# A two-block transformer layer on one core: three opening blocks made one, tiled load of x, gate product turned round, one modulation row moved

## The reference, cut to what matters

```python
xn = rmsnorm(x, norm1_g)                       # 256 x 2048
z = xn @ w_in                                  # columns: q, k, v, o (1024 each), 8 gates, u (1024)
q, k, v, o, gates, u = split(z)
gates = gates + b_gates                        # 256 x 8
...
dt = exp(log_dt); mag = exp(lam_re * dt)       # 64 groups x 64 states
ar, ai = mag * cos(lam_im * dt), mag * sin(lam_im * dt)
# x = u * B per group; a complex recurrence over the 256 tokens; y = Re(C * state) + d * u
ys = s5_groups(u, ...)                         # then a small gated product per group
mix = concat([mlstm(q, k, v, gates, o), ys]) @ w_out
...
# second block
mod = silu(c) @ w_ada + b_ada                  # one row of 6 * 2048, from a vector of 2048
```

## Time and profile before

| | |
|---|---|
| median of 3 runs | 3634.81 us (3632.55 to 3634.88) |
| the profiled execution, its own time | 3632.39 us |
| its span | 3630.5 us |
| busy share of the span: PE, DVE, POOL, ACT | 71%, 70%, 29%, 23% |
| mean HBM traffic | 283 GB/s |

### The profile page before, as it was taken

One profiled execution on the slowest core, in us unless ns is written; L12 is line 12 of the kernel. 1 busy time (PEld: TensorE's weight loads), 2 busy tenths in 40 slices (PEclk: granted clock), 3 DMA queues, 4 the chain that ended last, 5 costly groups with the idle time before them and its releaser, 6 DMA issues. The chain is left out here.

```text
span 3630.5 us, 27099 instructions
## 1 busy us (share of the span) xinstructions
PE 2592.8 (71%) x10406; PEld 1825.1 (50%) x10406; DVE 2542.4 (70%) x2541; ACT 835.7 (23%) x763; POOL 1060.7 (29%) x642
## 2 busy tenths in 40 slices
PE   7999899200165520006557999988899999999999
PEld 4444578100022200002224888767678788888887
DVE  3665647999899789987776787666746644444565
ACT  1001244000000000000002333344433433334333
POOL 1641000668867667885661000000000000000000
PEclk9999999655577665557777999989999999999999
DMA  6787355999999999999996898334466455555775
GB/s 200 254 304 278 128 194 203 372 372 417 418 422 422 411 406 422 422 422 422 421 421 257 314 321 290 134 122 142 139 223 244 162 188 194 186 185 192 259 260 191
DMA packets 332954, 1028.57 MB, mean 283 GB/s; under 512 B 36060, under 2 KB 36572, under 8 KB 265524
## 3 DMA queue, kind: packets, MB, share of 16 engines
q1 hardware_dynamic: 259124, 490.31, 39.0%
q0 software_dynamic: 73728, 536.90, 35.8%
HBM read 1020.29 MB, written 6.86 MB: 283 GB/s over the span
## 5 line engine op out<-in xcount | busy, mean ns | idle before, releaser
L387 DVE TENSOR_TENSOR slab_low<-ring,slab_high 128x2048 fp32r<-128x2048 f32 x240 | 550.0, 2292 | 522.5 <-ACT slab_high L380 522.3
L380 ACT CAST slab_high<-ring 128x2048 fp32r<-128x2048 f32 x304 | 580.1, 1910 | 1015.8 <-PE bank L366 800.5
L2238 PE MATMUL bank<-pool,upto 128*128 128x512 f32 x256 | 187.4, 901 | 658.9 <-ACT upto L2019 522.9
L1828 POOL DMA_INDIRECT pool<-in_peer_u,pool x256 | 509.9, 1992 | 413.3 <-DVE pool L1592 248.5
L364 PE MATMUL bank<-slab_high,left_high 128*128 128x512 f32 x1568 | 617.3, 394 | 11.4 <-DVE slab_low L387 7.6
L365 PE MATMUL bank<-slab_low,left_high 128*128 128x512 f32 x1568 | 613.4, 391 | 0.0
L366 PE MATMUL bank<-slab_high,left_low 128*128 128x512 f32 x1568 | 613.1, 391 | 0.0
L1638 DVE CUSTOM_DVE_ANT_0 pool<-pool,nat 128x2048 f32<-128x2048 f32 x248 | 558.6, 2289 | 30.1 <-DMA pool<-in_peer_u,pool 29.4
L1649 DVE SCALAR_TENSOR_TENSOR res<-pool,res 128x2048 f32<-128x2048 f32 x192 | 451.5, 2351 | 131.2 <-DMA pool<-in_peer_v,pool 115.7
L1828 POOL DMA_INDIRECT pool<-in_peer_v,pool x256 | 420.7, 1644 | 227.4 <-PE bank L2238 161.8
L2238 PEld LDWEIGHTS bank<-pool,upto 128*128 128x128 f32 x256 | 72.6, 298 | 774.3 <-issue 774.3
(11 more groups left out here) (577 smaller groups left out, 2923.1 us busy)
## 6 DMA issues: line engine op xcount, KB each, us to landing
ring<-in_w_in SPq DMA_DIRECT2D x140, 1024.0 KB, 5.0
ring<-in_w_ffn_in SPq DMA_DIRECT2D x88, 1024.0 KB, 4.9
ring<-in_w_ffn_out SPq DMA_DIRECT2D x44, 1024.0 KB, 5.1
ring<-in_w_ada SPq DMA_DIRECT2D x36, 1024.0 KB, 7.2
ring<-in_w_out SPq DMA_DIRECT2D x32, 1024.0 KB, 5.1
nat<-in_w_ada SPq DMA_DIRECT2D x64, 512.0 KB, 5.6
ring<-in_peer_wq SPq DMA_DIRECT2D x16, 1024.0 KB, 5.0
left_scratch<-in_w_ada SPq DMA_DIRECT2D x32, 512.0 KB, 5.6
```

What stands on the lines that cost most here:

```text
L380: nc.scalar.copy(high[:, n % PARTS], ring[:, g % SLOTS]).then_inc(high_done, 1)
L387: eng.tensor_tensor(dst, ring[:, g % SLOTS], high[:, n % PARTS].bitcast(F32), ALU.subtract)\
L1828: g.indirect_dma_start(dst, None, a[table][0], bass.IndirectOffsetOnAxis(idx[:, t, n:n + 1], 0))\
L2238: last = nc.tensor.matmul(ps[k][:, :], diagonals[sums_done(q, n) % 2], rows_[n % GB][:, k * NB:(k + 1) * NB], start=n == 0, stop=n == pe_r ...
```

## The change

The first three blocks and the S5 block become one block; the engines no longer meet between them, and each wait that a meeting had made needless is written out as a semaphore (`s_ra`, `s_rv`, `s_uc`, `s_cbc`, `s_prt`, `CONSTANTS`). Within it:

- x comes as two DMAs of 1 MB, one for each tile of 128 tokens, and the norm's weights are the next DMA, before the S5 rows and all slabs. The first slabs are u's columns. C, c, the gate columns, B and the small vectors come behind the first four slabs.
- ACT squares tile 0 and DVE tile 1 (a new multiply-and-sum). A square root of a constant at the very start loads ACT's table early. PE transposes tile 0 as soon as it is normed, tile 1 after it.
- The gate columns' product: weights are the 8 gate columns (padded to 32 with zeros), the moving operand is `raw_left` with 256 columns, 16 matmuls into four column groups of a bank. ACT copies the result (four partial sums on 128 partitions), and two small matmuls with `fold`, a stack of identities, add the parts and turn them back.
- The parameter rows' transposes stand after slab 1 of u, not after slab 3. `s_pow` is signalled behind the powers, before B's products. The gates' bias add moves behind B's masks.
- Modulation row 0 moves out of the norm's phase: `ROWS_S5` is 12 instead of 11, so 48 slabs of `w_ada` stand among the 24 projection slabs. silu(c) is made behind ACT's parameter work.

```diff
-        ROWS_NORM1, ROWS_S5 = 1, 11
-        FIRST_LATER = ROWS_NORM1 + ROWS_S5
+        ROWS_S5 = 12
+        FIRST_LATER = ROWS_S5
...
-        front = ada_slabs(0, 4 * ROWS_NORM1)
-        front += [("in", C_U + b * NB, j) for b in range(2) for j in range(4)]
+        front = [("in", C_U + b * NB, j) for b in range(2) for j in range(4)]
...
+                sp.dma_start(res[:, 0, :], x_tiles[0]).then_inc(s_xt[0], 16)
+                sp.dma_start(res[:, 1, :], x_tiles[1]).then_inc(s_xt[1], 16)
+                sp.dma_start(gain_row, a["norm1_g"][0].partition_broadcast(P)).then_inc(s_rows, 16)
...
+                for m in range(SLOTS):
+                    issue(sp, FRONT, m, m)
...
+                stream_on(sp, U0, U0 + 8)
+                sp.wait_ge(s_late, 64)
+                sp.wait_ge(s_prt, 1)
                 stream_on(sp, S0, O0)
...
+                    for t in range(TT):
+                        pe.wait_ge(s_nat, t + 1)
+                        for n in range(8):
+                            for j in range(2):
+                                k = 2 * n + j
+                                last = nc.tensor.transpose(ps[n][:, (2 * j + t) * P:(2 * j + t + 1) * P],
+                                                           nat[:, t, k * P:(k + 1) * P], ident[:, :])
...
+                    u_slabs(0, 2)
+                    pe.wait_ge(s_act, 4)
...
+                    u_slabs(2, 4)
+                    pe.wait_ge(s_wg, 16)
+                    for k in range(KD):
+                        i = k % 4
+                        last = nc.tensor.matmul(ps[5][32 * i:32 * i + 32, 0:T], wg[:, k, :], raw_left[:, k, :],
+                                                start=k < 4, stop=k >= KD - 4)
+                    last.then_inc(s_gpp, 1)
+                    pe.wait_ge(s_cm, 1)
+                    c_transposes(0, (6, 7))
+                    pe.wait_ge(s_gpc, 1)
+                    for t in range(TT):
+                        last = nc.tensor.matmul(ps[5][:, T + t * 8:T + t * 8 + 2 * H], gate_parts[:, t * P:(t + 1) * P],
+                                                fold[:, 0:2 * H], start=True, stop=True)
+                    last.then_inc(s_gpe, 1)
...
-                for t in range(TT):
-                    for k in range(KD):
-                        last = nc.tensor.matmul(ps[5][:, t * 8:t * 8 + 2 * H], raw_left[:, k, t * P:(t + 1) * P],
-                                                wg[:, k, :], start=k == 0, stop=k == KD - 1)
...
+                    dve.wait_ge(s_xt[1], 16)
+                    nc.vector.tensor_tensor_reduce(out=aTs[:, D:2 * D], in0=res[:, 1, :], in1=res[:, 1, :], scale=1.0, scalar=0.0,
+                                                   op0=ALU.mult, op1=ALU.add, accum_out=stat[:, 1:2]).then_inc(s_sqv, 1)
...
+                    act.wait_ge(s_one, 1)
+                    nc.scalar.activation(stat[:, 8:9], stat[:, 9:10], ACT.Sqrt)
+                    act.wait_ge(s_xt[0], 16)
+                    nc.scalar.activation(aTs[:, 0:D], res[:, 0, :], ACT.Square, accum_out=stat[:, 0:1]).then_inc(s_sq, 1)
...
-                v.tensor_tensor(mod_acc, mod_acc, ps[5][:, :], ALU.add)
+                    v.tensor_copy(mod_acc, ps[5][:, :])
```

More of the change, by code:

```diff
@@ L474, in build @@
         s_const = sem("constants")
[L475 to L521, removed]
@@ L633, in build @@
         more_slots.append(view(pool[:, place.at:place.at + SLAB], [KS, NB]))
-        row, wg = place.take(24, P), place.take(KD, 2 * H)
+        row = place.take(24, P)
         cw_at = place.at
@@ L652, in build @@
         b_raw = [early.take(TILES, HG) for _ in range(2)]
-        prod = [early.take(TILES, HG) for _ in range(2)]
+        beside = Places(aTs, KD * T)
+        prod = [beside.take(TILES, HG) for _ in range(2)]
+        wg, gate_parts, fold, c_row = beside.take(KD, 32), beside.take(T), beside.take(32), beside.take(KD)
+        gain_row = pool[:, 0:D]
         early = Places(parts_, 3 * D)
@@ L927, in _, with other_tables @@
+                def other_tables():
+                    g.wait_ge(s_bm, 1)
+                    for c in range(1, SC):
+                        if c >= 2:
+                            g.wait_ge(s_st, c - 1)
+                        tables(g, c)
+                constants()
+                first_tables()
+                other_tables()
             @block.tensor
             def _(pe):
-                def inputs(c):
-                    if c:
-                        pe.wait_ge(s_rot, c)
-                    for i in range(2):
-                        for b in range(TC):
-                            rows = slice(32 * b, 32 * b + 32)
-                            last = nc.tensor.matmul(ps[b][:, i * T:(i + 1) * T], BT[rows, c, i, :], uT[rows, c, :],
-                                                    start=True, stop=True)
-                    last.then_inc(s_xp, 1)
@@ L964, in _, with norm1 @@
[L964 to L975 removed]
+                def norm1():
+                    pe.wait_ge(s_const, CONSTANTS)
+                    for t in range(TT):
[5 more added lines that the diff above has]
+                                                           nat[:, t, k * P:(k + 1) * P], ident[:, :])
+                            if t == TT - 1:
+                                last.then_inc(s_tr, 1)
@@ new lines, in s5 @@
+                def s5():
+                    for b in range(IN_BLOCKS - 2):
+                        act.wait_ge(slabs_used, place_of["in", b * NB, 3] + 1)
+                        for t in range(TT):
+                            if b < 4:
+                                dst, src = nat[:, t, b * NB:(b + 1) * NB], ps[6 + t][:, :]
+                            else:
+                                hs = NB // DH
+                                dst = v_aug[:, t, (b - 4) * hs:(b - 3) * hs, 0:DH]
+                                src = view(ps[6 + t][:, :], [hs, DH])
+                            nc.scalar.copy(dst, src).then_inc(s_proj, 1)
```

717 lines of the change are left out of this document (348 added, 369 removed).

## The result

The changed kernel takes 3603.85 us (median of 6 runs, 3602.47 to 3605.37) against 3634.31 (median of 6, 3632.53 to 3638.44) on the same chip: ratio 0.9916, 95% interval 0.9904 to 0.9928, that is 30.5 us less. The forecast was 3605, and the gain lies where it was put: in PE's program of the first 320 us. The profiled execution took 3604.27 with a span of 3602.2.

The account below looks back on a forecast made before the run. PE's program was taken to bound the opening to the end of the S5 stage. -16.2 - 15.3 - 1.7 + 3.8 = -29.4 us against the median 3634.8 gave 3605.4, forecast 3605, range (8 in 10) 3599 to 3613.

Parts of the forecast that it names:

- from there to the S5 stage: PE from u's first slab to the S5 stage: 63.3 us instead of 78.6, -15.3.
- gate product: Gate columns' product before the S5 stage: 10.9 us becomes 1.8, plus 0.5 for two small matmuls, with no clock fall expected.
- first S5 slab, four more modulation slabs: S5 stage: first slab no longer cold, -1.7 us; four modulation slabs move in at 0.96 each, +3.8.
- norm's chain: Opening: weights and square both ready at 11.4, then passes and transposes; u's first slab at 19.2 instead of 35.40, -16.2 us.
- Rival 3: Behind the gate product and the small matmuls: the clock falls anyway, +2.9 us, 3608; chance 0.08.
- idle 3.90 us: PE's idle time at the meeting of engines ahead of the S5 stage: 3.90 us, forecast to go.
- tables: POOL's tables for the S5 stage: end by 83.6, at worst 90.8, in time for DVE's need at 92.6.
- contention with DVE's B work: POOL's table steps meet DVE's B products: POOL stands still up to 7.2 us; DVE can be held up to 7 us.
- parameter rows: DVE's parameter rows, for PE after two slabs of u: done at 30.2, needed by 33.1, cover 2.9 us.
- Rival 4: S5 stage: DMA becomes its bound and the kernel slower; at 260 GB/s 290 us, kernel 3659; chance 0.03.
- Rival 1: Ahead of u's first slab: TensorE starts cold, transposes don't raise the clock, 7.8 instead of 5.3 us; +4.4, 3610; chance 0.15.
- row: Modulation row 0 moved into the S5 stage: four slabs at 0.96 us each cost +3.8 there; they were free before.

Follow-up runs that it names:

- w_late: The changed kernel with the norm's weights issued behind the first four slabs of u instead of right behind x: 3614.41 us, ratio 0.9946.
- x_one: The changed kernel with x loaded as one DMA of 2 MB instead of two: 3605.91 us, ratio 0.9923.
- g_old: The changed kernel with only the gate columns' product turned back to 32 matmuls of 8 moving columns: 3613.90 us, ratio 0.9943.
- meet: The changed kernel with one meeting of all engines put back ahead of the S5 stage: 3605.04 us, ratio 0.9925.
- meet_p: The changed kernel with both the meeting ahead of the S5 stage and DVE's old order put back: 3612.48 us, ratio 0.9943.
- p_late: The changed kernel with DVE's old order: gates' bias add ahead of B's products, signal to POOL behind them: 3604.37 us, ratio 0.9922.
- best: The changed kernel with 22 idle matmuls ahead of the first transposes and DVE's second norm pass in two halves: 3603.57 us, ratio 0.9912.
- warm_t: The changed kernel with 36 idle transposes of a constant on PE ahead of the first transposes: 3602.46 us, ratio 0.9909.
- warm_m: The changed kernel with 22 idle matmuls on PE ahead of the first transposes: 3602.29 us, ratio 0.9911.
- row_front: The changed kernel with modulation row 0, c and silu(c) back in front of u's slabs, 44 w_ada slabs in the S5 stage: 3611.86 us, ratio 0.9945.
- g_split: The changed kernel with the old 8-column gate product in two halves, C's transposes and a slab of u between them: 3610.44 us, ratio 0.9934.
- wide4: The changed kernel with four instead of six slab buffers in the S5 stage: 3605.29 us (2 runs), ratio 0.9918.

## Why the prediction was right

Point by point, forecast against the trace of after:

| step | forecast | measured |
|---|---|---|
| DVE's first norm pass | 11.4 | 11.27 |
| u's first slab | 19.2, -16.2 | 19.48, -15.9 |
| from there to the S5 stage | 63.3, -15.3 | 63.26, -15.4 |
| of it the turned gate product and the two small ones | 1.8 + 0.5 | 1.87 + 0.37 |
| first S5 slab, four more modulation slabs | -1.7, +3.8 | stage 236.4 (forecast 236.9), from 234.8 |
| end of the S5 stage | -29.4 | -29.6 (348.80 to 319.17) |
| the median | -29.4 | -30.5 |

No step of the table is off by more than 0.5 us. That the median comes within 1.2 us of the forecast is partly luck, since single executions differ by more: the spans of the two profiled ones differ by 28.3, because the same code behind the S5 stage took 1.3 us longer in the one after.

The **norm's chain** was right in size and nearly in its cause: weights and square were forecast to meet at 11.4; the weights came at 10.9 and the square, which took 2.29 us as one pass of its shape, ended last. `w_late` shows that the weights' place decides, `x_one` that the tiles of x do not. The term that was a little off is the transposes: 5.3 forecast, 5.88 measured, and 5.28 to 6.58 over the runs with this opening.

The **gate product** and the clock: with the new form there is no fall of the clock, and `g_old` brings it back. Its price of 9.7 us in the opening is less than the 11.4 that the rows of before gave, as the old product ran 4.2 us at the higher clock this time instead of 3.0, and its fall ended sooner. Rival 3 is out.

The **idle 3.90 us** were counted right, but put down to the meeting; the prediction read that the tables ended just ahead of the S5 stage and drew nothing from it. `meet` and `meet_p` show that the meeting costs PE 1.9 us, and the rest comes when POOL's tables stand in front of it. Two parts of the change, the new order on DVE and the merged block, each take this wait away by themselves (`meet`, `p_late`), so neither can claim it alone. The **tables** start at 41.05 and their first chunk ends at 78.06, 14 us ahead of need. The contention with DVE's B work is there, and in this work on POOL's side only. POOL's timeline, and two rows of DVE's from the S5 stage:

```profile
41.05 0.15 POOL L640 MEMSET parts_scratch<- 128x32 f32 x1 [35.10 <-DVE res L953]
...
45.37 1.22 POOL L646 TENSOR_TENSOR parts_scratch<-parts_scratch,res 128x64 f32<-128x64 f32 x1
...
57.45 0.30 POOL L646 TENSOR_TENSOR parts_scratch<-parts_scratch,res 128x64 f32<-128x64 f32 x1
```

```profile
98.88 1.22 DVE L1009 TENSOR_TENSOR pool<-pool,res 128x1024 f32<-128x1024 f32 x1
...
116.41 2.94 DVE L1009 TENSOR_TENSOR pool<-pool,res 128x1024 f32<-128x1024 f32 x1
```

The same step takes 1.22 us beside DVE's work and 0.30 without it; the near tables take 14.5 us (41.05 to 55.59), the far ones 10.2. DVE's B work takes 6.8 us (40.84 to 47.67), as long as before (74.78 to 81.55). In the S5 stage, beside POOL's long table steps, DVE is held up too: the same operation takes 2.94 us there, as it did before the change, and 1.22 while POOL is idle. The Trainium skill's rule (SBUF — State Buffer, Who interferes with whom), by which either side can block the other, goes with both losses; that DVE's B work would be held up by up to 7 us did not show.

The cover of DVE's **parameter rows** was forecast at 2.9 us and is 2.8 (30.52 against 33.31). In `best`, where u's first slab starts at 17.18, the rows end at 28.3 and PE comes at 31.01: the cover travels along, because DVE's program starts from the same transposes.

**Rival 4**, DMA as the bound of the S5 stage, is out: 318 GB/s at a share of 0.89 with PE busy throughout, and even four buffers suffice. **Rival 1** was wrong about the transposes, which do raise the clock (`warm_t`), and right in that they start at the lower one; against warm ones this costs 1.7 us (`warm_m`), but the forecast's 5.3 had most of it in, so of the rival's 4.4 only 0.3 came about (19.48 against 19.2). Here the Trainium skill (TensorE: Matmul & The Clock Gate, Part 4: PE-mode transpose) and the measurement differ: it says that transposes don't count as busy for the gate (its figures beside this are for bf16, these transposes are fp32); after 36 idle transposes the next 16 took 0.12 us each, half of the 0.244 in the earlier trace rows. The measurement decides.

That +3.8 for the moved **row** was a price worth paying is shown by `row_front`: in front of u's slabs the row delays them by 11.1 us and saves 3.4 in the S5 stage.

## What to carry to other kernels

A meeting of all engines costs little by itself: ahead of the S5 stage PE went on 0.5 to 0.7 us after the last engine's work had ended (POOL's before and in `meet_p`, DVE's copies in `meet`). What it costs is the slowest engine's lag, put on the path of the bound one. Look for the engine that arrives last, and for what its program waits for, before crediting the merge. In an opening, order the DMA queue by what the first bound engine needs: one transfer of 1 MB behind four others cost 10.6 us. And this product with its narrow moving operand cost the busy TensorE twice, in its own time and in the clock of what follows; with the narrow matrix as weights, packed in column groups, both go.

## What the runs showed of the hardware that was not expected

The first 32 transposes, the first work of TensorE in the kernel, took 5.28, 5.61, 5.67, 5.88, 6.13, 6.43 and 6.58 us in traces with the same opening. With 22 idle matmuls ahead of them they took 3.71 where DVE's passes let them (`best`). With four modulation slabs ahead, 0.7 to 0.8 us of idle time between these, they took 4.75 (`row_front`); the slabs themselves took 1.94 us each there, against 1.07 in the S5 stage, so they had not raised the clock. So the clock's rise comes at a place that differs from run to run, by up to 1.3 us of time. PE in two stretches of the changed kernel's transposes (length, busy, PEclk, DMA share, GB/s):

```profile
17.00:18.00 1.00, 1.00 (x6) 1.00 1.05 385
18.00:19.00 1.00, 1.00 (x10) 1.00 1.04 383
```

The PEclk column shows 1.00 in both, although the first holds 6 transposes and the second 10: ahead of the first change that the trace records, the column is no evidence, and durations have to be read.

The clock fell behind 3.5 us of narrow matmuls and 0.9 us of transposes in `g_split` and did not behind the other 3.5 us. An idle time of TensorE of 1.69 us left the next slab at 7.11 us, 3.90 and 7.75 us made it 8.80 and 8.74. But a short one is not safe either. At the end of the S5 stage TensorE is idle for 1.74 to 1.79 us in every trace. In five of the fourteen (after, `g_old`, `g_split`, `w_late`, `wide4`) the clock then fell for a few us (in after PEclk is 0.51 from 322 to 325), in nine it did not. PE's timeline of after:

```profile
321.14 2.83 PE L2047 MATMUL bank<-ident,nat 128*128 128x128 f32 x16
323.76 7.89 PE L354 MATMUL bank<-ring,left_scratch 128*128 128x512 f32 x16
```

In `meet` the same two rows are 1.97 and 7.03. This is 1.7 us of a kernel's time that no edit here touches.
